# First block's gates: SiLU by ScalarE's table replaced by tanh on ScalarE and a product on VectorE, inside the attention

## Chip, core and metric

The kernel runs on one core of one Trainium2 chip. The metric is the time of one execution in microseconds (us). Engines are TensorE (PE; its weight loads are PEld), VectorE (DVE), ScalarE (ACT), GpSimd (POOL), and SyncE (SP), which issues most DMAs.

## What is computed

Two transformer-like blocks on 512 tokens of width 1024, in float32. Only the end of the first block's mixing matters here:

```python
y_ssm  = s5_mixer(ssm_u, ...) * jax.nn.silu(ssm_z)            # 512 x 512
y_attn = dsa_mixer(q, k, v, q_idx, k_idx, w_idx, ...) * jax.nn.silu(attn_z)   # 512 x 512
y = jnp.concatenate([y_ssm, y_attn], axis=-1) @ w_out[l]
x = x + gate[:, None, :] * y
```

`s5_mixer` is a state space layer that ends in `z * sigmoid(z @ w_glu + b_glu)`; `dsa_mixer` is causal attention with 8 heads of 64 over the 128 keys that an indexer selects for each query. `silu(v)` is `v * sigmoid(v)`, which is also `0.5 * v * (1 + tanh(v / 2))`.

## The kernel before

Activations lie feature-major: 128 features on the partitions, 512 tokens along the free dimension; a tile of that shape is a chunk. Each float32 product is made of three TensorE passes over numbers split into a high and a low part (`w_hi`, `w_lo`; `h_hi`, `h_lo`; `y_hi`, `y_lo`), all by the one matmul helper at L575. Weights come as 1 MB tiles through three buffers `w_raw`; ScalarE rounds a tile to `w_hi`, VectorE subtracts to get `w_lo`. A group is one such tile: two halves of 128 output features, each 24 matmuls of 128x512 into one PSUM bank. Groups rotate through three banks (`GEMM_BANKS`), and `bank_free` tells TensorE that a bank has been read. Nothing is scheduled by a planner: every engine's order is written out by hand, and semaphores tie the engines together.

**The stage of the change** is one loop of 16 steps, j = 0 to 15, that overlaps the attention with the products `attn_z` and `ssm_z`. Step j serves two heads for query tile j // 4, so its keys are 128 wide in steps 0 to 3, 256 in 4 to 7, 384 in 8 to 11 and 512 in 12 to 15.

- TensorE, in step j: `logits(j+1)` (matmuls `bank<-k,q`), `transposes(j)` (L954), which wait for the normalised probabilities, `values(j-1)` (`bank<-pT,v`), then 4 units of the gate products (3 units from step 8 on); a unit is three matmuls. Half 0 of the eight gate halves is done ahead of the loop, the other seven inside. After it come `values(15)` and `out1`, the product with `w_out`, whose first half waits for each of its eight inputs `y` in turn by `counts=(4, 5, 6, 7, 8, 8, 8, 8)` on the number of low parts that are written.
- VectorE, in step j: waits until the exponentials of step j exist, takes reciprocals (L2385), scales the two heads' probabilities (L2387), and then for step j+1 adds the bias to the logits (L2326) and masks them (L2330). Behind these four come the side jobs of the step: two quarters of a weight tile's low part in steps 0, 1, 4, 5, 8, 9, 13 and 14 (`gate_low`, L2340), one round of key selection (`select_keys`, L2208 and L2209) in steps 2, 3, 6 and 7, the products with the gates (`attn_gated`, L2360) in steps 9 and 12, and low parts (L1987) in steps 10 and 13. The four `ssm_gated` (L2373) and their low parts stand behind the loop, and so do those of the last query tile.
- ScalarE, in step j: exponentials for step j+1 (L1546), copies of the turned probabilities (`pT`, L1555), and side jobs: `gate_half` (L1576) copies a finished gate half out of its bank in steps 0, 2, 4, 6, 8, 11, 14 and 15 and frees the bank; `gate_high` rounds half a weight tile (L1567); `gate_silu` (L1582) applies SiLU in place, four chunks `az` at the end of step 7, three chunks `sz` in step 14 and the fourth behind the loop; `high` and `attn_high` write `y_hi`.

The eight inputs of `out1` pass through two buffers `tval`, in the order given by `Y_SSM` and `Y_ATTN`: value a may be written once the low part of value a-2 is done (`new_val`).

```python
Y_SSM, Y_ATTN = [3, 4, 5, 6], [0, 1, 2, 7]
GATE_DONE = {0: 0, 2: 1, 4: 2, 6: 3, 8: 4, 11: 5, 14: 6, 15: 7}   # step: gate half copied there
GATE_LOW  = {0: ..., 1: ..., 4: ..., 5: ..., 8: ..., 9: ..., 13: ..., 14: ...}
```

Of the kernel before, what the change touches and what calls it, by code (L numbers as in the profile page):

```python
# [114 lines left out]
AT = {}  # L115
# [3 lines left out]
    _at += _n  # L119


Y_SSM, Y_ATTN = [3, 4, 5, 6], [0, 1, 2, 7]


def y_ssm(m):

    return AT["y"] + Y_SSM[m]
# [37 lines left out]
def hybrid_blocks(nc, wstream, xT, vecs, consts, head_rows, onehot, rel_bias, ssm_vec, ssm_b, ssm_c, d_skip,  # L165
                  alpha2, decay, reset, outT):
    f32, f32r, i32 = mybir.dt.float32, mybir.dt.float32r, mybir.dt.int32
    ALU, ACT, AX = mybir.AluOpType, mybir.ActivationFunctionType, mybir.AxisListType
# [10 lines left out]
    with ctx:  # L179
# [14 lines left out]
        def sem(name):  # L194
            return ctx.enter_context(nc.semaphore(name))
# [28 lines left out]
        sgb = sb("sgb", [P, 2, SEQ])  # L224
# [64 lines left out]
        bank = [ctx.enter_context(nc.psum_tensor(f"bank{i}", [P, SEQ], f32)) for i in range(8)]  # L289
# [9 lines left out]
        bank_free = [sem(f"bank_free{i}") for i in range(8)]  # L299

        act_val, act_high, act_low = sem("act_val"), sem("act_high"), sem("act_low")
# [5 lines left out]
        cl_zero, bias_spread = sem("cl_zero"), sem("bias_spread")  # L307
        kr_turned, kr_row = sem("kr_turned"), sem("kr_row")
        ki_copied, ki_doubled, wi_ready, wi_row, wi_psum, mod_row, gate_row = sem("ki_copied"), sem("ki_doubled"), sem("wi_ready"), sem("wi_row"), sem("wi_psum"), sem("mod_row"), sem("gate_row")
        az_ready = sem("az_ready")  # L310
        x_act, kr_psum, k_ready, heads_loaded = sem("x_act"), sem("kr_psum"), sem("k_ready"), sem("heads_loaded")
        silu_zero, c_ready, ada_done, mod_ready = sem("silu_zero"), sem("c_ready"), sem("ada_done"), sem("mod_ready")
        setup_trig, trig_ready = sem("setup_trig"), sem("trig_ready")
# [50 lines left out]
        def pbanks(gr):  # L364
            return bank_of(2 * gr.g), bank_of(2 * gr.g + 1)
# [99 lines left out]
        GATE_HALVES = [(gr, half) for name in ("attn_z", "ssm_z") for gr in G[name] for half in range(2)]  # L465
# [5 lines left out]
        GATE_DONE = {0: 0, 2: 1, 4: 2, 6: 3, 8: 4, 11: 5, 14: 6, 15: 7}  # L471
# [101 lines left out]
        def _(pe):  # L573
# [60 lines left out]
            def gemm(gr, kind, hi, lo, k0=0, permuted=False, need=None, between=None, counts=None):  # L634

                gemm_half(gr, 0, kind, hi, lo, k0, permuted, need, counts=counts)
                if between is not None:
                    between()
                gemm_half(gr, 1, kind, hi, lo, k0, permuted, need)
# [236 lines left out]
            gr = G["k"][1]  # L876
# [106 lines left out]
                    unit += 1  # L983
            values(15)
            for w, gr in enumerate(G["out1"]):
                gemm(gr, "fm", y_hi, y_lo, need=AT["y"] if w == 0 else None, counts=(4, 5, 6, 7, 8, 8, 8, 8),
                     between=(lambda: presummed("norm1")) if w == 3 else None)
            pe.wait_ge(pv_read, 4)

# [280 lines left out]
        def _(act):  # L1270
            steps = 0

            def settle(ins):

                nonlocal steps
                steps += 1
                ins.then_inc(act_step, 1)
                act.wait_ge(act_step, steps)
# [289 lines left out]
                if part == 1:  # L1568
                    ins.then_inc(w_high, 1)

            def gate_half(n):

                gr, half = GATE_HALVES[n]
                bk = pbanks(gr)[half]
                act.wait_ge(group_done, 2 * gr.g + half + 1)
                settle(act.copy((az, sz)[n // 4][:, n % 4, :], bank[bk][:, :]))  # L1576
                act.nop().then_inc(bank_free[bk], 1)

            def gate_silu(x, ms):

                for m in ms:
                    ins = act.activation(x[:, m, :], x[:, m, :], ACT.Silu)  # L1582
                ins.then_inc(az_ready, 1)

            def attn_kept(qt):

# [4 lines left out]
            def attn_high(qt):  # L1591

                a = y_attn(qt)
                act.wait_ge(act_val, a + 1)
                act.copy(y_hi[:, 4:8, qt * P:qt * P + P],
                         tval[:, a % 2, :].rearrange("p (c q) -> p c q", q=P)).then_inc(act_high, 1)

            def ssm_high(m):

                high(y_ssm(m), y_hi[:, m, :])  # L1600
# [5 lines left out]
            for j in range(16):  # L1606
                for r in range(2):
                    if j + 1 < 16:
                        probabilities(2 * j + 2 + r)
                    turned_copy(2 * j + r)  # L1610
                if j == 4 or j == 8:
                    attn_kept(j // 4 - 1)
                if j == 15:
                    ssm_high(0)
                    ssm_high(1)
                if j in GATE_DONE:
                    gate_half(GATE_DONE[j])
                if j in GATE_HIGH:
                    gate_high(*GATE_HIGH[j])
                if j == 7:  # L1620
                    gate_silu(az, range(4))
                if j == 9:
                    attn_high(0)
                    attn_high(1)
                if j == 12:
                    attn_high(2)
                if j == 14:
                    gate_silu(sz, range(3))
            gate_silu(sz, (3,))
            ssm_high(2)  # L1630
            ssm_high(3)
            attn_high(3)

# [269 lines left out]
        def _(dve):  # L1903
# [9 lines left out]
            def tt(out, a, b, op):  # L1913
                settle(dve.tensor_tensor(out, a, b, op))  # L1914
# [5 lines left out]
            def stt(out, a, s, b, op0, op1):  # L1920
                settle(dve.scalar_tensor_tensor(out=out, in0=a, scalar=s, in1=b, op0=op0, op1=op1))  # L1921
# [57 lines left out]
            def new_val(a):  # L1979

                if a >= 2:
                    dve.wait_ge(act_low, a - 1)
                return tval[:, a % 2, :]
# [316 lines left out]
            for w, gr in enumerate(G["glu"]):  # L2300
                ahead(gr)
                for half in range(2):
                    m = 2 * w + half
                    if m < 3:
                        select_keys(1)
                    if m == 1:
                        dve.wait_ge(ada_done, 6)
                        dve.tensor_tensor(modv[:, 16:24], bank[4][:, 0:8], vec[:, a0 + 16:a0 + 24], ALU.add)\
                           .then_inc(mod_ready, 1)
                    dve.wait_ge(sig_ready, m + 1)  # L2310
                    tt(z32[:, m, :], sgb[:, m % 2, :], z32[:, m, :], ALU.mult)
                    dve.nop().then_inc(sig_used, 1)
            dve.wait_ge(mod_ready, 5)
            dve.nop().then_inc(copied_dve, 3)
# [30 lines left out]
            def by_tile(x):  # L2345

                return x.rearrange("p (c q) -> p c q", q=P)

            def attn_gated(qt):

                rows = slice(qt * P, qt * P + P)
                dve.wait_ge(az_ready, 1)
                a = y_attn(qt)
                if qt < 2:
                    dve.wait_ge(pv_read, qt + 1)
                    out = q32[:, :, rows]
                else:
                    dve.wait_ge(pv_psum, 8 * qt + 8)
                    out = by_tile(bank[PV_BANK][:, :])
                dve.tensor_tensor(by_tile(new_val(a)), out, az[:, :, rows], ALU.mult).then_inc(act_val, 1)  # L2360
                if qt >= 2:
                    dve.wait_ge(act_val, a + 1)
                    dve.nop().then_inc(pv_read, 1)

            def attn_low(qt):

                rows, a = slice(qt * P, qt * P + P), y_attn(qt)
                low(a, y_lo[:, 4:8, rows], y_hi[:, 4:8, rows], by_tile(tval[:, a % 2, :]))

            def ssm_gated(m):  # L2370

                dve.wait_ge(az_ready, 2 + m // 3)
                dve.tensor_tensor(new_val(y_ssm(m)), z32[:, m, :], sz[:, m, :], ALU.mult).then_inc(act_val, 1)  # L2373

            def ssm_low(m):

                low(y_ssm(m), y_lo[:, m, :], y_hi[:, m, :])
# [3 lines left out]
            for j in range(16):  # L2381
                i = 2 * j
                qt = i // 8
                dve.wait_ge(p_exp, i + 2)
                settle(dve.reciprocal(stat[:, 3, i:i + 2], stat[:, 2, i:i + 2]))  # L2385
                for r in range(2):
                    dve.tensor_scalar(prob(i + r, qt), prob(i + r, qt), stat[:, 3, i + r:i + r + 1], None,  # L2387
                                      ALU.mult).then_inc(p_norm, 1)
                if j + 1 < 16:
                    masked_logits(i + 2)  # L2390
                    masked_logits(i + 3)
                for part in GATE_LOW.get(j, ()):
                    gate_low(*part)
                if j in (2, 3, 6, 7):
                    select_keys(1)
                if j == 9:
                    attn_gated(0)
                    attn_gated(1)
                if j == 10:
                    attn_low(0)  # L2400
                    attn_low(1)
                if j == 12:
                    attn_gated(2)
                if j == 13:
                    attn_low(2)
            for m in range(4):
                ssm_gated(m)
                if m:
                    ssm_low(m - 1)
            attn_gated(3)  # L2410
            ssm_low(3)
            attn_low(3)
# [492 lines left out]
```

## Time and profile before

| | us |
|---|---|
| median of 3 runs (lowest, highest) | 1520.94 (1519.44, 1521.02) |
| the profiled execution's own time | 1518.23 |
| its span in the trace | 1516.4 |
| TensorE busy | 1481.4 |
| VectorE busy | 828.1 |
| ScalarE busy | 604.1 |

The span is what the trace covers; 1.8 us of that execution lie around it. The profiled execution is 2.7 us under the median. A timeline row reads: start, duration, engine, line, operation, what is written and read, shapes, and how many instructions the row merges; in brackets the engine's idle time ahead of it and what ended that. The name of a line can be that of a helper. A window row gives the busy time of each engine in a stretch and `PEclk`, the granted TensorE clock as a share of full speed.

### The profile page before, as it was taken

The page shows a single profiled execution, that of the slowest core. Times are in us where ns is not written, and L with a number is a line of the kernel's source. Part 1 is how long each engine was busy: PE and PEld are TensorE (multiplying, and loading weights), DVE is VectorE, ACT ScalarE, POOL GpSimd, SP SyncE. Part 2 cuts the span into 40 slices and gives each one's busy share as a digit, 9 for nine tenths or more (in the row PEclk, how much of TensorE's full clock was granted, in tenths as well). Part 3 has the DMA queues.
Part 4 walks back from the last instruction along what each step waited for, and adds up shares of the span by engine and source line. Part 5 has one row for each costly group of instructions (what it writes and reads, how often), then busy time and mean ns, then how long its engine had stood idle before and what let it go on. Part 6 is the DMA issues. An engine that isn't in the chain of part 4 may idle for free.

```text
span 1516.4 us, 19843 instructions
## 1 busy us (share of the span) xinstructions
PE 1481.4 (98%) x8104; PEld 1202.5 (79%) x8104; DVE 828.1 (55%) x1359; ACT 604.1 (40%) x918; POOL 22.2 (1%) x39
## 2 busy tenths in 40 slices
PE   7999999999999999999999999999999999999997
PEld 5766967678887887888889777888887888888887
DVE  7978978865647663334346443543448544443234
ACT  4356335663336553334336434332434323232220
POOL 0020100000000000000000000000000000000000
PEclk9999999999999999999999999999999999999998
DMA  8541542043321112122222212222421323232221
GB/s 344 183 112 57 116 161 90 29 167 139 111 80 61 56 56 73 66 84 84 98 105 86 82 56 84 84 98 97 149 101 57 110 84 112 83 111 77 104 98 56
DMA packets 25001, 151.69 MB, mean 100 GB/s; under 512 B 3568, under 2 KB 6240, under 8 KB 8896
## 3 DMA queue, kind: packets, MB, share of 16 engines
q1 hardware_dynamic: 22304, 136.71, 24.9%
q0 software_dynamic: 2608, 13.72, 3.4%
q8 instruction: 64, 1.05, 0.3%
q14 instruction: 25, 0.20, 0.0%
HBM read 143.83 MB, written 7.88 MB: 100 GB/s over the span
## 4 chain that ended last, share of the span: by engine, by line
PE 89%; DVE 6%; ACT 2%; DMA 2%; issue 1%; SPq 0%; DVEq 0%; ACTq 0%
PE bank L575 87%; DMA w_raw<-wstream 2%; PE bank L1022 1%; PE bank L954 1%; DVE score L2224 1%; DVE tmp L1914 0%; DVE w_lo L1961 0%; DVE win_im L1914 0%; DVE win_re L1914 0%; DVE sgb L1921 0%; DVE y_lo L1987 0%; DVE h_lo L1987 0%; DVE tval L2461 0%; ACT w_hi L1291 0%; DVE score L2209 0%
## 5 line engine op out<-in xcount | busy, mean ns | idle before, releaser
L575 PE MATMUL bank<-h_hi,w_hi 128*128 128x512 f32 (+1 forms) x1104 | 438.6, 397 | 5.3 <-DVE h_lo L2743 2.1
L575 PE MATMUL bank<-h_hi,w_lo 128*128 128x512 f32 (+1 forms) x1120 | 437.3, 390 | 0.0
L575 PE MATMUL bank<-h_lo,w_hi 128*128 128x512 f32 (+1 forms) x1104 | 430.9, 390 | 0.0
L1961 DVE TENSOR_TENSOR w_lo<-w_raw,w_hi 128x2048 fp32r<-128x2048 f32 (+2 forms) x104 | 234.6, 2255 | 250.6 <-ACT w_hi L1291 249.3
L1291 ACT CAST w_hi<-w_raw 128x2048 fp32r<-128x2048 f32 (+2 forms) x108 | 202.7, 1876 | 139.0 <-PE bank L575 132.5
L575 PEld LDWEIGHTS bank<-h_hi,w_hi 128*128 128x128 f32 (+1 forms) x1104 | 207.3, 188 | 61.7 <-issue 17.1
L575 PEld LDWEIGHTS bank<-h_hi,w_lo 128*128 128x128 f32 (+1 forms) x1120 | 210.4, 188 | 45.1
L575 PEld LDWEIGHTS bank<-h_lo,w_hi 128*128 128x128 f32 (+1 forms) x1104 | 207.3, 188 | 41.7 <-issue 0.2
L575 PE MATMUL bank<-y_hi,w_hi 128*128 128x512 f32 x272 | 108.9, 400 | 1.9 <-DVE y_lo L1987 1.9
L575 PE MATMUL bank<-y_hi,w_lo 128*128 128x512 f32 x272 | 106.1, 390 | 0.0
L575 PE MATMUL bank<-y_lo,w_hi 128*128 128x512 f32 x272 | 105.9, 389 | 0.0
L575 PE MATMUL bank<-w_hi,h_hi 128*128 128x256 f32 x352 | 101.3, 288 | 0.0
L575 PE MATMUL bank<-w_lo,h_hi 128*128 128x256 f32 x352 | 99.5, 283 | 0.0
L575 PE MATMUL bank<-w_hi,h_lo 128*128 128x256 f32 x352 | 99.5, 283 | 0.0
L1661 ACT ACTIVATE sgb<-bank 128x512 f32<-128x512 f32 x40 | 23.9, 598 | 151.0 <-PE bank L575 151.0
L575 PE MATMUL bank<-f_hi,w_lo 128*128 128x512 f32 (+1 forms) x220 | 76.2, 347 | 0.0
L575 PEld LDWEIGHTS bank<-w_hi,h_hi 128*128 128x128 f32 x352 | 67.4, 191 | 6.2 <-issue 6.1
L575 PE MATMUL bank<-f_hi,w_hi 128*128 128x512 f32 (+1 forms) x196 | 69.8, 356 | 0.0
L575 PE MATMUL bank<-f_lo,w_hi 128*128 128x512 f32 (+1 forms) x196 | 69.4, 354 | 0.0
L575 PEld LDWEIGHTS bank<-w_lo,h_hi 128*128 128x128 f32 x352 | 67.5, 192 | 0.0
L575 PEld LDWEIGHTS bank<-w_hi,h_lo 128*128 128x128 f32 x352 | 67.5, 192 | 0.0
L575 PEld LDWEIGHTS bank<-y_hi,w_hi 128*128 128x128 f32 x272 | 51.1, 188 | 16.3 <-DVE y_lo L1987 3.6
(401 smaller groups left out, 1817.5 us busy)
## 6 DMA issues: line engine op xcount, KB each, us to landing
w_raw<-wstream SPq DMA_DIRECT2D x119, 1024.0 KB, 4.8
w_raw<-wstream SPq DMA_DIRECT2D x4, 768.0 KB, 4.1
bias_rows<-bias_table POOLq DMA_DIRECT2D x1, 2560.0 KB, 11.2
xr<-xT SPq DMA_DIRECT2D x4, 512.0 KB, 5.0
bias<-bias_rows POOLq DMA_DIRECT2D x1, 2048.0 KB, 12.8
xr<-xT SPq DMA_DIRECT2D x1, 2048.0 KB, 8.7
x_saved<-xr POOLq DMA_DIRECT2D x1, 2048.0 KB, 10.4
xr<-x_saved POOLq DMA_DIRECT2D x1, 2048.0 KB, 8.1
```

The source lines that it names most:

```text
L575: return pe.matmul(out, lhsT, rhs, start=start, stop=stop)
L954: ins = pe.transpose(bank[PT_BANKS[r]][:, s * P:s * P + P], prob(i, qt)[:, s * P:s * P + P], ident)
L1022: ins = pe.transpose(bank[ST_BANKS[t % 2]][:, j * P:j * P + P], lg[:, n % 2, j, kb * P:kb * P + P], ident)
L1291: act.copy(hi_of(s)[:, 0:kt, :], w_raw[:, i % RAW_SLOTS, 0:kt, :]).then_inc(w_high, 1)
L1661: act.activation(sgb[:, m % 2, :], bank[bk][:, :], func).then_inc(bank_free[bk], 1)
L1961: dve.tensor_tensor(w_low_of(s)[:, 0:kt, :], w_raw[:, i % RAW_SLOTS, 0:kt, :], hi_of(s)[:, 0:kt, :].bitcast(f32), ALU.subtract).then_inc(w ...
L2224: dve.scalar_tensor_tensor(out=score[:, qt, 0:w], in0=sgb[:, i % 2, 0:w], scalar=wi[:, qt, h:h + 1], in1=score[:, qt, 0:w], op0=ALU.mult, ...
```

## The change

ScalarE no longer copies the gate halves and applies SiLU later. `gate_tanh` writes `tanh(v / 2)` straight from the bank in the same steps in which the copy stood; the SiLU activations of this stage are gone. VectorE's new `gate_silu` computes `(tanh + 1) * v` with the bank as second input, one step later (steps 1, 3, 5, 7, 9, 12 and 15, and once behind the loop), and frees the bank. The factor 0.5 goes into `attn_gated` and, for the state space chunks, into the product that ends `s5_mixer`; both become scalar-tensor-tensor operations. The rounds of key selection stand in steps 1, 3, 5 and 7 instead of 2, 3, 6 and 7. `ssm_gated(0)` and `(1)` and their low parts move into steps 11 to 14, so two more of the eight inputs of `out1` are ready when the loop ends, and the `tval` order and the first of the `counts` follow.

```diff
--- before.py
+++ after.py
@@ -119,7 +119,7 @@
     _at += _n
 
 
-Y_SSM, Y_ATTN = [3, 4, 5, 6], [0, 1, 2, 7]
+Y_SSM, Y_ATTN = [2, 4, 5, 6], [0, 1, 3, 7]
 
 
 def y_ssm(m):
...
@@ -983,7 +983,7 @@
                     unit += 1
             values(15)
             for w, gr in enumerate(G["out1"]):
-                gemm(gr, "fm", y_hi, y_lo, need=AT["y"] if w == 0 else None, counts=(4, 5, 6, 7, 8, 8, 8, 8),
+                gemm(gr, "fm", y_hi, y_lo, need=AT["y"] if w == 0 else None, counts=(3, 5, 6, 7, 8, 8, 8, 8),
                      between=(lambda: presummed("norm1")) if w == 3 else None)
             pe.wait_ge(pv_read, 4)
 
@@ -1568,19 +1568,12 @@
                 if part == 1:
                     ins.then_inc(w_high, 1)
 
-            def gate_half(n):
+            def gate_tanh(n):
 
                 gr, half = GATE_HALVES[n]
-                bk = pbanks(gr)[half]
                 act.wait_ge(group_done, 2 * gr.g + half + 1)
-                settle(act.copy((az, sz)[n // 4][:, n % 4, :], bank[bk][:, :]))
-                act.nop().then_inc(bank_free[bk], 1)
-
-            def gate_silu(x, ms):
-
-                for m in ms:
-                    ins = act.activation(x[:, m, :], x[:, m, :], ACT.Silu)
-                ins.then_inc(az_ready, 1)
+                act.activation((az, sz)[n // 4][:, n % 4, :], bank[pbanks(gr)[half]][:, :], ACT.Tanh, scale=0.5)\
+                   .then_inc(tanh_ready, 1)
 
             def attn_kept(qt):
 
@@ -1610,24 +1603,21 @@
                     turned_copy(2 * j + r)
                 if j == 4 or j == 8:
                     attn_kept(j // 4 - 1)
-                if j == 15:
-                    ssm_high(0)
-                    ssm_high(1)
                 if j in GATE_DONE:
-                    gate_half(GATE_DONE[j])
+                    gate_tanh(GATE_DONE[j])
                 if j in GATE_HIGH:
                     gate_high(*GATE_HIGH[j])
-                if j == 7:
-                    gate_silu(az, range(4))
                 if j == 9:
                     attn_high(0)
                     attn_high(1)
+                if j == 11:
+                    ssm_high(0)
                 if j == 12:
                     attn_high(2)
-                if j == 14:
-                    gate_silu(sz, range(3))
-            gate_silu(sz, (3,))
-            ssm_high(2)
+                if j == 13:
+                    ssm_high(1)
+                if j == 15:
+                    ssm_high(2)
             ssm_high(3)
             attn_high(3)
 
@@ -2308,7 +2298,7 @@
                         dve.tensor_tensor(modv[:, 16:24], bank[4][:, 0:8], vec[:, a0 + 16:a0 + 24], ALU.add)\
                            .then_inc(mod_ready, 1)
                     dve.wait_ge(sig_ready, m + 1)
-                    tt(z32[:, m, :], sgb[:, m % 2, :], z32[:, m, :], ALU.mult)
+                    stt(z32[:, m, :], sgb[:, m % 2, :], 0.5, z32[:, m, :], ALU.mult, ALU.mult)
                     dve.nop().then_inc(sig_used, 1)
             dve.wait_ge(mod_ready, 5)
             dve.nop().then_inc(copied_dve, 3)
@@ -2349,7 +2339,7 @@
             def attn_gated(qt):
 
                 rows = slice(qt * P, qt * P + P)
-                dve.wait_ge(az_ready, 1)
+                dve.wait_ge(az_ready, 4)
                 a = y_attn(qt)
                 if qt < 2:
                     dve.wait_ge(pv_read, qt + 1)
@@ -2357,7 +2347,8 @@
                 else:
                     dve.wait_ge(pv_psum, 8 * qt + 8)
                     out = by_tile(bank[PV_BANK][:, :])
-                dve.tensor_tensor(by_tile(new_val(a)), out, az[:, :, rows], ALU.mult).then_inc(act_val, 1)
+                dve.scalar_tensor_tensor(out=by_tile(new_val(a)), in0=out, scalar=0.5, in1=az[:, :, rows],
+                                         op0=ALU.mult, op1=ALU.mult).then_inc(act_val, 1)
                 if qt >= 2:
                     dve.wait_ge(act_val, a + 1)
                     dve.nop().then_inc(pv_read, 1)
@@ -2369,8 +2360,18 @@
 
             def ssm_gated(m):
 
-                dve.wait_ge(az_ready, 2 + m // 3)
+                dve.wait_ge(az_ready, 5 + m)
                 dve.tensor_tensor(new_val(y_ssm(m)), z32[:, m, :], sz[:, m, :], ALU.mult).then_inc(act_val, 1)
+
+            def gate_silu(n):
+
+                gr, half = GATE_HALVES[n]
+                bk, x = pbanks(gr)[half], (az, sz)[n // 4][:, n % 4, :]
+                dve.wait_ge(tanh_ready, n + 1)
+                dve.scalar_tensor_tensor(out=x, in0=x, scalar=1.0, in1=bank[bk][:, :], op0=ALU.add,
+                                         op1=ALU.mult).then_inc(az_ready, 1)
+                dve.wait_ge(az_ready, n + 1)
+                dve.nop().then_inc(bank_free[bk], 1)
 
             def ssm_low(m):
 
@@ -2391,7 +2392,9 @@
                     masked_logits(i + 3)
                 for part in GATE_LOW.get(j, ()):
                     gate_low(*part)
-                if j in (2, 3, 6, 7):
+                if j - 1 in GATE_DONE:
+                    gate_silu(GATE_DONE[j - 1])
+                if j in (1, 3, 5, 7):
                     select_keys(1)
                 if j == 9:
                     attn_gated(0)
@@ -2399,14 +2402,20 @@
                 if j == 10:
                     attn_low(0)
                     attn_low(1)
+                if j == 11:
+                    ssm_gated(0)
                 if j == 12:
+                    ssm_low(0)
                     attn_gated(2)
                 if j == 13:
                     attn_low(2)
-            for m in range(4):
-                ssm_gated(m)
-                if m:
-                    ssm_low(m - 1)
+                    ssm_gated(1)
+                if j == 14:
+                    ssm_low(1)
+            ssm_gated(2)
+            gate_silu(GATE_DONE[15])
+            ssm_gated(3)
+            ssm_low(2)
             attn_gated(3)
             ssm_low(3)
             attn_low(3)
```

## Rows read from the trace of the kernel before

**Rows 1.** The page: chain that ended last, shares by engine

```profile
PE 89%; DVE 6%; ACT 2%; DMA 2%; issue 1%; SPq 0%; DVEq 0%; ACTq 0%
```

**Rows 2.** Windows: the loop up to step 9, and one microsecond in step 9

```profile
240.00:280.00 40.00, 40.00 (x221) 27.33 (x221) 32.72 (x101) 24.36 (x64) 0.00 (x0) 1.00 0.15 54
...
283.00:284.00 1.00, 1.00 (x8) 0.67 (x8) 0.96 (x4) 0.20 (x2) 0.00 (x0) 0.50 0.00 0
```

**Rows 3.** Timeline of PE, from 247 to 324 us

```profile
247.91 0.44 PE L954 MATMUL bank<-cst,sgb 128*128 128x128 f32 x2
...
279.60 0.92 PE L575 MATMUL bank<-k,q 64*128 64x384 f32 x4
282.52 1.16 PE L954 MATMUL bank<-cst,sqb 128*128 128x128 f32 x6 [2.00 <-DVE sqb L2387]
...
287.95 0.92 PE L575 MATMUL bank<-k,q 64*128 64x384 f32 x4
...
292.67 1.13 PE L575 MATMUL bank<-k,q 64*128 64x512 f32 x4
...
303.82 1.09 PE L954 MATMUL bank<-cst,sqb 128*128 128x128 f32 x8
...
309.26 1.09 PE L954 MATMUL bank<-cst,sgb 128*128 128x128 f32 x8
...
314.25 1.09 PE L954 MATMUL bank<-cst,sqb 128*128 128x128 f32 x8 [0.61 <-DVE sqb L2387]
...
318.57 1.09 PE L575 MATMUL bank<-pT,v 128*64 128x128 f32 x16
...
323.98 0.50 PE L575 MATMUL bank<-y_hi,w_hi 128*128 128x512 f32 x1 [0.70 <-DVE y_lo L1987]
```

**Rows 4.** Timeline of ACT, from 275 to 279 us: table changes

```profile
275.33 1.28 ACT L1582 ACT_TABLE_LOAD   x1
...
278.83 1.28 ACT L1546 ACT_TABLE_LOAD   x1
```

**Rows 5.** Timeline of DVE, from 246 to 324 us

```profile
246.27 0.16 DVE L2385 RECIPROCAL stat<-stat 128x2 f32<-128x2 f32 x1
...
282.71 0.61 DVE L2326 SCALAR_TENSOR_TENSOR sgb<-bank,stat,bias 128x384 f32<-128x384 f32 x1
...
287.38 0.15 DVE L2385 RECIPROCAL stat<-stat 128x2 f32<-128x2 f32 x1
...
302.53 0.17 DVE L2385 RECIPROCAL stat<-stat 128x2 f32<-128x2 f32 x1 [0.28 <-ACT sqb L1546]
...
308.53 0.15 DVE L2385 RECIPROCAL stat<-stat 128x2 f32<-128x2 f32 x1
...
313.52 0.15 DVE L2385 RECIPROCAL stat<-stat 128x2 f32<-128x2 f32 x1
...
322.40 0.69 DVE L2360 TENSOR_TENSOR tval<-bank,az 128x512 f32<-128x512 f32 x1
323.23 1.29 DVE L1987 TENSOR_TENSOR y_lo<-tval,y_hi 128x512 fp32r<-128x512 f32 x2
```

**Rows 6.** Groups by line and shape over the whole span (busy us, mean ns)

```profile
L1921 DVE SCALAR_TENSOR_TENSOR la<-la,lb 128x512 f32<-128x512 f32 x4 | 2.8, 693 | 4.8 <-ACT lb L1804 4.8
...
L1661 ACT ACTIVATE sgb<-bank 128x512 f32<-128x512 f32 x40 | 23.9, 598 | 151.0 <-PE bank L575 151.0
```

**Rows 7.** Groups by line and shape of DVE, 232 to 326 us

```profile
L2208 DVE MAX8 small<-score 128x8 f32<-128x512 f32 x5 | 3.4, 688 | 0.0
L2209 DVE MATCH_REPLACE8 score<-small,score 128x512 f32<-128x512 f32 x5 | 3.4, 677 | 0.0
...
L2387 DVE TENSOR_SCALAR sgb<-sgb,stat 128x128 f32<-128x128 f32 x4 | 1.0, 283 | 0.1
```

**Rows 8.** Waits of PE over the whole span (total, times, longest)

```profile
PE bank L575 <- DVE h_lo L2743: 2.1, 1, 2.1
PE bank L575 <- DVE w_lo L1961: 1.9, 1, 1.9
```

More of the change, by code:

```diff
@@ L309, in hybrid_blocks @@
         ki_copied, ki_doubled, wi_ready, wi_row, wi_psum, mod_row, gate_row = sem("ki_copied"), sem("ki_doubled"), sem("wi_ready"), sem("wi_row"), sem("wi_psum"), sem("mod_row"), sem("gate_row")
-        az_ready = sem("az_ready")
+        tanh_ready, az_ready = sem("tanh_ready"), sem("az_ready")
         x_act, kr_psum, k_ready, heads_loaded = sem("x_act"), sem("kr_psum"), sem("k_ready"), sem("heads_loaded")
```

## The prediction

> **What bounds the kernel now.** I read the chain that ended last first: 89% of it is TensorE [rows 1], so a change outside TensorE counts only where it removes or adds a pause of TensorE. The windows show which engine is next: in the 40 us up to step 9 TensorE is busy all the time and VectorE 32.7 us, 82%, ScalarE 24.4 us [rows 2]. The reserve is VectorE's, and it is thin. Then TensorE's timeline, step by step, with VectorE's beside it. In three places TensorE pauses in or just behind this loop.
>
> Step 9: its transposes start after 2.00 us of idleness, at 282.52, and from one logits to the next it takes 287.95 - 279.60 = 8.35 us, where the following step takes 292.67 - 287.95 = 4.72 [rows 3]. So 3.63 us are lost: 2.00 idle, and some 1.6 because the granted clock then stands at 0.50, the lower of its two levels (1.2 instead of 2.4 GHz) [rows 2]. The cause is ScalarE: a table load of 1.28 us at 275.33, four SiLU, another load at 278.83 [rows 4], and the exponentials for step 9 behind them. Step 15: 314.25, idle 0.61, some 0.65 late by the row before; this one is VectorE's doing. Behind the loop: from the last `values` at 318.57 to the fourth input of `out1` at 323.98 it is 5.41 us [rows 3], where 1.03 for the values and three units of 0.68 would be 3.1.
>
> **What goes.** The SiLU block of step 7 and both loads round it: 3.63 us, if nothing takes its place. The copy out of the bank becomes a tanh out of the bank; the nearest row, another function from bank to SBUF, takes 0.598 [rows 6], as the copy did, and it lies beside other work.
>
> **What comes, on VectorE.** `gate_silu` is a scalar-tensor-tensor with an immediate; such a one over 512 columns takes 0.693 [rows 6], and with the wait for its own end I charge 0.73. One with its second input in a bank and an immediate scalar is not in the trace; the bounds are 0.60 (the pitch of back-to-back operations, half of the 1.29 of two [rows 5]) and 0.80; I take 0.73. A round of selection is 0.688 + 0.677 [rows 7] and a small load between, 1.51 in all. A moved `ssm_gated` or low part costs 0.60 of VectorE's time.
>
> What counts is when the first head of step j+1 is normalised, against when TensorE comes to its transposes. From the start of the reciprocal to those transposes it takes 314.25 - 313.52 = 0.73 us in steps where TensorE waits [rows 3, 5]; with 128 columns the scaling is 0.283 [rows 7], so about 0.55. Side jobs added ahead of the reciprocal move it one for one once the reserve is used.
>
> Step 1: before, the reciprocal starts at 246.27 [rows 5], the result is there at 246.82, TensorE comes at 247.91 [rows 3]: reserve 1.09. Added: 0.73 + 1.51 = 2.24. Pause **1.15**. Three more steps are read in the same way from their own pairs of rows: step 3, reserve 0.36, added 0.73, pause **0.37**; step 5, reserve 1.04, added 2.24, pause **1.20**; step 7, reserve 0.0, added 0.73, pause **0.73**. Taking a selection round out of steps 2 and 6 gives nothing back, since they had reserve.
>
> Step 9 has to be rebuilt, as its rows are disturbed. VectorE goes from first bias to reciprocal in 287.38 - 282.71 = 4.67 us [rows 5], with two gate_low parts and two `attn_gated`. It can begin some 0.94 after the logits start (their 0.92 us [rows 3]). So 0.94 + 4.67 + 0.68 = 6.29 after the logits, and TensorE comes to the transposes 4.72 + 0.86 = 5.58 after them: late by 0.71 already, once the SiLU block no longer hides it. With `gate_silu` 0.73 more: **1.44**.
>
> Step 11: one `ssm_gated`, covered by VectorE's wait for ScalarE there. Step 12: the reciprocal starts at 302.53 after 0.28 of idleness [rows 5], so VectorE was free at 302.25; plus 0.73 + 0.60, then 0.73, is 304.31, against 303.82 [rows 3]: **0.49**. Step 13: the reciprocal at 308.53 and the transposes at 309.26 [rows 3, 5] touch already; added is one `ssm_gated`, 0.60, and 0.16 since VectorE now begins the step late: **0.76**. Step 14: pause 0.65 before, a low part of 0.60 more: **1.25**.
>
> The sum: 1.15 + 0.37 + 1.20 + 0.73 + 1.44 + 0.49 + 0.76 + 1.25 = 7.39 us of pauses in place of 3.63 + 0.65 = 4.28. The loop gets 3.1 us longer.
>
> **Behind the loop** something comes back. Count from the last `values` (318.57 before). Half 7 has just ended; the tanh, no longer behind SiLU work, runs from 0.1 to 0.7, `gate_silu` to 1.45, `ssm_gated(3)` to 2.15, and low part 2 ends at 2.8. `attn_gated(3)` waits for that and starts at 2.9; its spacing to the next low part was 323.23 - 322.40 = 0.83 [rows 5], so low part 3 ends at 4.45 and TensorE takes the fourth input at 4.5, the rest at 5.2 without another wait. Before it was 5.41: **0.9** less. The next weight tile of `out1` is rounded behind this and has some 4 us to spare, and the reload of `x` starts as soon as the last logits are masked, as before; both move with the loop.
>
> Net: 7.39 - 4.28 - 0.9 = **+2.2 us**. Against the profiled execution: span 1516.4 to 1518.6, its own time 1518.23 to 1520.4. The median of the runs is 2.7 us above that execution, so 1520.94 + 2.2 = **1523.1**. About 0.2%, 3.0 us, is what a measurement of this kernel can tell from no change, so this lies inside it.
>
> The products that end `s5_mixer` and `attn_gated` change from tensor-tensor to scalar-tensor-tensor with an immediate: 0.693 against 0.69 for `attn_gated` in the timeline [rows 5, 6], nothing. The Trainium skill (Vector Engine (DVE) Microarchitecture Reference, section Points that are easy to get wrong) says that a scalar-tensor-tensor with two non-bf16 inputs in SBUF runs at half throughput. Rows 6 are such an operation at 693 ns, so the trace speaks against it; by that rule the two `attn_gated` of step 9 would cost 1.4 us more and the sum would be +3.6.
>
> **Rivals.**
>
> *VectorE's additions fit in.* If the reserve is larger than I read, as when the reciprocal's chain overlaps better, the pauses of the loop vanish and the gain stays: -3.63 - 0.9 to -5.2 with step 15's, so 1515.7 to 1516.4. It decides at step 1: the selection round and the gate together would have to fit into 1.1 us [rows 3, 5]. Against it stands that step 15 pauses before by the very sum that I use. 0.08.
>
> *The clock falls.* A pause may bring the granted clock down again, at 1.6 us each time. Before, 2.00 us did [rows 2, 3]; elsewhere TensorE waits up to 1.9 and 2.1 us [rows 8]. My longest are 1.44, 1.25 and 1.20, in steps 9, 14 and 5. One fall gives 1524.7, two 1526.3: slower. It decides if one of them comes near 2 us. 0.15.
>
> *tanh needs a table of its own.* Then the loads do not go but multiply: two of 1.28 us [rows 4] around each tanh. ScalarE idles for some 1.7 us ahead of the exponentials, and VectorE's extra work hides more; the rest shows in step 12 (about 0.8) and the last tanh's load behind the loop (1.3): 1525.2. For the whole change not to do what it says it would have to be this. 0.05. The Trainium skill (ScalarE: Activation LUTs, section Table sets: the hidden batching unit) lists tanh in the set of exp, which would exclude this; no run so far shows it.
>
> **How the numbers follow.** The forecast itself has 0.72. Its unknowns are the price of `gate_silu` (0.60 to 0.80 at six counting places: -0.8 to +0.4), the estimate of step 9 (0.3 either way), and the runs of before, which differ by 1.6 us among themselves. So its own range is 1521 to 1525, and of its 0.72 some 0.20 lies over +3.0. Faster 0.07, same 0.52, slower 0.20 + 0.15 + 0.05 and rounding, 0.41. The range takes in the falls of the clock: 1520.8 to 1526.4.
>
> **What the profile will show.** No table load between the one ahead of the loop and the one for the square root. No 2.00 us pause in step 9, and steps 1, 5, 9, 13 and 14 each with TensorE's transposes waiting for L2387 of VectorE by 0.8 to 1.4 us; those would say that VectorE is the bound. VectorE near 90% busy in the loop. `out1`'s first two inputs back to back. If the transposes of step 2 start without a wait, my reading of the reserves is wrong; if the granted clock shows 0.50 in the loop, the second rival is at work.

## The result and the profile after

| | before | after |
|---|---|---|
| median of 14 runs each, us (lowest, highest) | 1519.07 (1517.06, 1521.70) | 1522.66 (1521.38, 1524.07) |
| ratio to before, 95% interval | | 1.0022 (1.0015 to 1.0030) |
| profiled execution, its own time, us | 1518.23 | 1524.07 |
| its span, us | 1516.4 | 1522.3 |

The change makes the kernel slower by 1.5 to 3.0 per thousand, 3.4 us at the middle (the medians lie 3.59 apart); 2.2 were forecast. (With 14 runs the median of before is 1.9 us lower than that of the three runs shown at first.)

TensorE's timeline of the changed kernel, at the places that answer to [rows 3]; in brackets is the idle time ahead of a row and what ended it:

```profile
242.38 0.49 PE L575 MATMUL bank<-k,q 64*128 64x128 f32 x4
242.80 0.44 PE L954 MATMUL bank<-cst,sgb 128*128 128x128 f32 x2
...
250.07 0.49 PE L575 MATMUL bank<-k,q 64*128 64x128 f32 x4
251.75 0.52 PE L954 MATMUL bank<-cst,sgb 128*128 128x128 f32 x2 [1.18 <-DVE sgb L2388]
...
260.95 0.70 PE L954 MATMUL bank<-cst,sgb 128*128 128x128 f32 x4 [0.40 <-DVE sgb L2388]
...
271.55 0.70 PE L954 MATMUL bank<-cst,sgb 128*128 128x128 f32 x4 [1.13 <-DVE sgb L2388]
...
282.43 0.88 PE L954 MATMUL bank<-cst,sgb 128*128 128x128 f32 x6 [0.78 <-DVE sgb L2388]
...
290.83 0.92 PE L575 MATMUL bank<-k,q 64*128 64x384 f32 x4
293.34 0.88 PE L954 MATMUL bank<-cst,sgb 128*128 128x128 f32 x6 [1.60 <-DVE sgb L2388]
...
309.15 1.09 PE L954 MATMUL bank<-cst,sqb 128*128 128x128 f32 x8 [0.69 <-DVE sqb L2388]
...
315.35 1.09 PE L954 MATMUL bank<-cst,sgb 128*128 128x128 f32 x8 [0.73 <-DVE sgb L2388]
...
320.94 1.09 PE L954 MATMUL bank<-cst,sqb 128*128 128x128 f32 x8 [1.18 <-DVE sqb L2388]
...
325.25 1.09 PE L575 MATMUL bank<-pT,v 128*64 128x128 f32 x16
326.28 0.50 PE L575 MATMUL bank<-y_hi,w_hi 128*128 128x512 f32 x1
...
327.08 0.40 PE L575 MATMUL bank<-y_hi,w_hi 128*128 128x512 f32 x1
...
329.91 0.50 PE L575 MATMUL bank<-y_hi,w_hi 128*128 128x512 f32 x1 [0.70 <-DVE y_lo L1977]
```

The pause of 2.00 us in step 9 that ScalarE made is gone. In its place TensorE pauses at eight points, seven of them new and the one of step 15 grown from 0.61 to 1.18 us idle, and each is ended by L2388, VectorE's scaling of the probabilities. They stand ahead of the transposes of steps 2, 4, 6, 8, 10, 13, 14 and 15: in each case one step behind the step that got more side jobs. What TensorE loses at one is a little more than the idle time shown: the transposes start 1.68 us after the logits ahead of them where they otherwise start 0.42 after (242.80 - 242.38), so 1.26 are lost at the first. Read in this way the eight are 1.26, 0.47, 1.21, 0.85, 1.67, 0.76, 0.80 and 1.25 us, 8.27 in all.

VectorE's timeline in step 1 shows the cause. It is the stretch that ended with the reciprocal at 246.27 in [rows 5]:

```profile
247.65 1.29 DVE L2330 TENSOR_TENSOR w_lo<-w_raw,w_hi 128x512 fp32r<-128x512 f32 x2
248.86 0.68 DVE L2371 SCALAR_TENSOR_TENSOR az<-az,bank 128x512 f32<-128x512 f32 x1
249.69 0.69 DVE L2198 MAX8 small<-score 128x8 f32<-128x512 f32 x1
250.41 0.09 DVE L2199 MATCH_VALUE_LOAD score<-small,score 128x8 f32 x1
250.49 0.68 DVE L2199 MATCH_REPLACE8 score<-small,score 128x512 f32<-128x512 f32 x1
251.20 0.17 DVE L2386 RECIPROCAL stat<-stat 128x2 f32<-128x2 f32 x1
```

The gate's product takes 0.68 us and occupies the engine for 0.83 (249.69 - 248.86), since VectorE waits for its end to signal the bank. Without it and the selection round the reciprocal would start at 248.86. Two windows of the changed kernel, columns as in [rows 2]: the steps up to 9, and steps 12 to 14.

```profile
242.00:293.00 51.00, 46.25 (x256) 30.79 (x255) 42.16 (x123) 26.21 (x74) 0.00 (x0) 1.00 0.12 42
303.00:321.00 18.00, 15.40 (x106) 10.41 (x104) 17.31 (x38) 11.76 (x24) 0.00 (x0) 1.00 0.10 22
```

In the first VectorE is busy 83% of the time, in the second 96% (TensorE 91% and 86%). The granted clock is 1.00 in both, so 2.4 GHz, and in the microseconds between them too: no pause of the loop brought it down. The table load for the exponential stands at 237.21, ahead of the loop, and the next one, for the square root, at 329.68; tanh and the exponential run between them without a load, so both are served by the same table (grouped by line, 238 to 329 us, a window that still catches the end of the first load):

```profile
L1575 ACT ACTIVATE az<-bank 128x512 f32<-128x512 f32 x4 | 2.4, 600 | 0.0
...
L1595 ACT ACT_TABLE_LOAD x1 | 1.3, 1283 | 0.2 <-ACT sgb L1539 0.2
```

From the second logits to the fourth input of `out1` the changed kernel takes 329.91 - 242.38 = 87.53 us, before 84.19 (323.98 - 239.79): 3.34 more. That is the measured change. The second logits of the kernel before start here:

```profile
239.79 0.49 PE L575 MATMUL bank<-k,q 64*128 64x128 f32 x4
```

The other 2.6 us by which the two profiled spans differ lie ahead of the loop, where the changed kernel's trace has the granted clock at its lower level twice, near 29 and 70 us, and that of before not at all; a second trace of the kernel before has one of them too, near 68 us, and starts the loop 1 us later. From the fourth input on the two traces agree to 0.1 us.

### The profile page after: what moved, and what is told of

Its sections match the earlier page's. It is cut to its first block, busy times and chain, and to the rows that moved or that the text cites. A ratio compares the mean times of both kernels' runs of the same rounds, so it can differ in the third digit from the quotient of the medians.

```text
span 1522.3 us, 19840 instructions
## 1 busy us (share of the span) xinstructions
PE 1484.0 (97%) x8104; PEld 1204.2 (79%) x8104; DVE 832.9 (55%) x1367; ACT 595.7 (39%) x907; POOL 22.1 (1%) x39
## 4 chain that ended last, share of the span: by engine, by line
PE 88%; DVE 7%; ACT 2%; issue 1%; DMA 1%; SPq 0%; DVEq 0%; ACTq 0%
PE bank L575 86%; DMA w_raw<-wstream 1%; PE bank L1022 1%; DVE score L2214 0%; DVE score L2199 0%; DVE sgb L2316 0%; DVE w_lo L2330 0%; DVE small L2198 0%; PE bank L954 0%; DVE tmp L1904 0%; DVE w_lo L1951 0%; DVE win_im L1904 0%; DVE win_re L1904 0%; DVE sgb L1911 0%; DVE h_lo L1977 0%
```

## Experiments

The stretch above, from the second logits to the fourth input of `out1`, is called the stretch; for the two kernels that were traced twice it repeats within 0.1 us (84.19 and 84.16; 86.53 and 86.61), so it resolves what the timed ratios, with intervals of some 2 per thousand, do not.

### Selection back to steps 2, 3, 6 and 7

```diff
-                if j in (1, 3, 5, 7):
+                if j in (2, 3, 6, 7):
                     select_keys(1)
```

> The changed kernel with the rounds of key selection back in steps 2, 3, 6 and 7. If VectorE's side jobs ahead of the reciprocal make the pauses one for one: the pauses ahead of the transposes of steps 2 and 6 (1.18 and 1.13 us idle in the changed kernel) are gone, since 1.21 + 0.83 fits the reserve of some 2.3 us of a step, steps 2 and 6 themselves stay without a pause in steps 3 and 7 of TensorE, and the loop is 2.4 us shorter than in the changed kernel, about 1 us longer than before: ratio to before 1.0007. If the pauses come from the gates' products alone (their banks, their place), the move does nothing: ratio 1.002 as for the changed kernel.

Ratio 1.0016 (1.0007 to 1.0026). The pauses ahead of the transposes of steps 2 and 6 are gone and the six others stayed within 0.02 us: 5.80 instead of 8.27. The stretch is 84.97 us, 2.56 less than in the changed kernel and 0.78 more than before. Here are TensorE's rows in place of those at 250.07 and 251.75:

```profile
247.59 0.49 PE L575 MATMUL bank<-k,q 64*128 64x128 f32 x4
248.01 0.44 PE L954 MATMUL bank<-cst,sgb 128*128 128x128 f32 x2
```

So by the stretch, putting back the selection rounds alone, which had been moved by one step, from steps with room to steps without, undoes 2.56 of the net 3.34 us. It removes 2.47 of the 8.27 us of pauses; the pauses gone from steps 9 and 15 (4.28) and the shorter way behind the loop (0.75) pay for 5.0 of the 5.80 that are left. The timed runs do not show the 2.56: 0.78 us more than before would be a ratio of 1.0005, just under the interval of 1.0007 to 1.0026, while 1.0016 is near the 1.002 that the other case in the expectation gave. The trace decides that the two pauses went, and its execution was, with 1518.97 us, the fastest of the ten. What the other nine lost is not known.

### State space chunks behind the loop

```diff
-Y_SSM, Y_ATTN = [2, 4, 5, 6], [0, 1, 3, 7]
+Y_SSM, Y_ATTN = [3, 4, 5, 6], [0, 1, 2, 7]
...
-                if j == 11:
-                    ssm_gated(0)
...
+            ssm_gated(0)
+            ssm_gated(1)
+            ssm_low(0)
             ssm_gated(2)
+            ssm_low(1)
             gate_silu(GATE_DONE[15])
             ssm_gated(3)
```

> The changed kernel with the state space chunks gated and split behind the loop, as before, but ahead of the last gate_silu. If side jobs count one for one: the pauses ahead of the transposes of steps 13, 14 and 15 shrink by 0.6 us each (0.76, 0.80, 1.25 to about 0.15, 0.15, 0.65), and nothing is paid behind the loop, since VectorE is idle for 3.2 us there: 1.8 us less than the changed kernel, ratio to before about 1.001. If the early chunks are what shortens the way from the last values to the fourth input of out1 (5.41 to 4.66 us), that comes back and takes 0.75 us of it: ratio 1.0015.

> The same kernel as ssm_behind, for a second trace. Its timed ratio of 1.003 is above the 1.0015 that its loop and tail account for. If falls of the granted clock near 326 and 442 us belong to this kernel, they show again; if they fall at random, at least one of the two is absent, and the pauses of the loop are the same as in the first trace to 0.05 us.

Ratio 1.0030 (1.0019 to 1.0041). The loop did as expected: the pauses for steps 13, 14 and 15 are 0.25, 0.23 and 0.64 us (second trace 0.24, 0.23, 0.65), 1.69 less. But from the last values to the fourth input it takes 5.42 us again (5.44), as before and not 4.66, so in this order of VectorE the early chunks are what shortens that way. They are not the only means: the kernel before without SiLU takes 4.73 us with no chunk moved, and the kernel of the fifth experiment 4.65 with only the first chunk in step 15. What the changed kernel adds behind the loop, the last `gate_silu`, is what the early chunks make up for here. VectorE's rows show why the way is long in this kernel: it idles 1.38 us behind the first two chunks, because ScalarE rounds the first only after its two last copies of probabilities, and `gate_silu(7)` starts 0.8 us after its tanh is done.

```profile
317.73 1.29 DVE L2363 TENSOR_TENSOR tval<-z,sz 128x512 f32<-128x512 f32 x2 [0.21 <-DVE sz L2370]
320.40 0.69 DVE L1976 TENSOR_TENSOR y_lo<-tval,y_hi 128x512 fp32r<-128x512 f32 x1 [1.38 <-ACT y_hi L1299]
```

And there is a cost I had not expected. TensorE waits 1.08 us and then 0.68 for the third and fourth input; at the fourth the granted clock falls, in both traces:

```profile
324.65 0.50 PE L575 MATMUL bank<-y_hi,w_hi 128*128 128x512 f32 x1 [1.08 <-DVE y_lo L1976]
...
326.31 0.79 PE L575 MATMUL bank<-y_hi,w_hi 128*128 128x512 f32 x1 [0.68 <-DVE y_lo L1976]
326.90 0.63 PE L575 MATMUL bank<-y_lo,w_hi 128*128 128x512 f32 x1
```

A window over a microsecond of it has 0.50:

```profile
327.00:328.00 1.00, 1.00 (x4) 0.80 (x3) 0.00 (x0) 0.96 (x3) 0.56 (x1) 0.50 0.06 25
```

From the fourth input to the first product after the second block's last norm, 814.7 us in the kernels before and after, it takes 816.3 us in the second trace, where this is the only fall: 1.6 more. With the stretch of 86.61, 2.4 more than before, it makes 4.0 us more than before, 1.0026, inside the interval. The fall near 442 us in the first trace is absent from the second, so that one does not belong to the kernel.

### The gates' products left out

```diff
-                dve.scalar_tensor_tensor(out=x, in0=x, scalar=1.0, in1=bank[bk][:, :], op0=ALU.add,
-                                         op1=ALU.mult).then_inc(az_ready, 1)
-                dve.wait_ge(az_ready, n + 1)
+                dve.nop().then_inc(az_ready, 1)
```

> The changed kernel without VectorE's eight products of tanh + 1 and the bank: the gates stay tanh, so that part of the computation is left out. By the forecast's sum each product costs TensorE 0.85 us wherever the reserve is used up: pauses of about 0.4, 0, 0.35, 0, 0.75 us ahead of the transposes of steps 2, 4, 6, 8 and 10, 0 for step 13, 0.6 to 0.8 for 14 and 1.25 for 15; the loop is some 4.5 us shorter than in the changed kernel and the way behind it 0.7 shorter: ratio to before about 0.9985. If instead the tanh or ScalarE's new order sets the pauses, they stay, and the ratio is above 1.001.

Ratio 0.9994 (0.9985 to 1.0004). The pauses are 0.42, 0, 0.38, 0.02 and 0.71 us for steps 2, 4, 6, 8 and 10, 0 for 13, then 0.73 and 1.25: 3.5 in all, every one within 0.05 of what was expected (with 0.85 us for a product, the price read in the changed kernel, not the forecast's 0.73). The stretch is 82.13 us, 2.06 less than before. ScalarE's tanh and its new order therefore cost nothing that shows in the loop; VectorE's eight products of 0.83 us account for 4.8 of the 8.27. (The shares of products, selection rounds and chunks, 4.8, 2.5 and 1.7, add up to more than 8.27, since they use up the same reserves.) The ratio is less good than the stretch alone would make it (0.9986), though inside the interval. This trace has one more fall of the clock, near 437 us; that the other runs had it too is not shown.

### The kernel before without SiLU

```diff
-                for m in ms:
-                    ins = act.activation(x[:, m, :], x[:, m, :], ACT.Silu)
-                ins.then_inc(az_ready, 1)
+                act.nop().then_inc(az_ready, 1)
```

> The kernel before, with ScalarE's eight SiLU (and with them their table loads) left out, so the gates are not SiLU. The pause of 2.00 us ahead of the transposes of step 9 and the fall of the granted clock behind it go. By the forecast's rebuilding of step 9 a pause of 0.7 us then shows ahead of the transposes of step 10, hidden before; without it the step before takes 4.7 us. So the loop gains 3.6 - 0.7 = 2.9 us, and what stands behind it some 1 us: ratio 0.9975. A rival: the 0.7 is not there and the gain is 3.6 + 1: ratio 0.997.

> The kernel before, for a second trace. If the pause of 2.00 us in step 9 always brings the clock down, step 9 takes 8.35 us again; if not, it takes some 6.8.

Ratio 0.9976 (0.9966 to 0.9985). Step 9 takes 4.72 us instead of 8.35, and a pause appears that the trace before did not have: TensorE loses 0.74 us ahead of the transposes of step 10, where 0.71 had been worked out. The stretch is 80.64 us, 3.55 less than before: 3.63 - 0.74 in the loop and 0.68 behind it, where some 1 us had been expected. This is the whole value of taking SiLU off ScalarE with every other job left in its place, at a price of nothing. The second trace of the kernel before has the pause (1.99 us) and the fall of the clock in step 9 again.

### Side jobs placed by the reserve of each step

```diff
+        SILU_AT = {1: 0, 4: 1, 5: 2, 6: 3, 10: 4, 12: 5, 15: 6}
...
-                if j - 1 in GATE_DONE:
-                    gate_silu(GATE_DONE[j - 1])
-                if j in (1, 3, 5, 7):
+                if j in (2, 3, 6, 7):
                     select_keys(1)
+                if j == 15:
+                    ssm_gated(0)
+                if j in SILU_AT:
+                    gate_silu(SILU_AT[j])
                 if j == 9:
                     attn_gated(0)
-                    attn_gated(1)
                 if j == 10:
-                    attn_low(0)
-                    attn_low(1)
+                    attn_gated(1)
                 if j == 11:
-                    ssm_gated(0)
+                    attn_low(0)
+                    attn_low(1)
```

The rest of the chunks stand behind the loop as in the second experiment, and on ScalarE `ssm_high(0)` goes ahead of the last two copies and `attn_high(1)` into step 10.

> The changed kernel with every side job of VectorE placed by the reserve of its step: selection in 2, 3, 6, 7; gate_silu 0 to 6 in steps 1, 4, 5, 6, 10, 12, 15; attn_gated 0 and 1 in 9 and 10, their low parts in 11; the state space chunks behind the loop, the first rounded ahead of the last copies of ScalarE. If the reserve is what counts (about 2.3, 2.3, 1.9, 2.1, 2.3, 2.3, 2.0, 1.5, 1.7, 1.9, 1.3, 1.5, 1.7, 0.7 us in steps 1 to 14), the pauses ahead of the transposes come to 0.1 to 0.2 us in steps 10, 13 and 14 and 0.6 in 15, 1.1 in all instead of 8.3, and with 4.7 us from the last values to the fourth input of out1 the stretch from the second logits to there is 80.4 us (before 84.2, changed 87.5): ratio 0.9975. If tanh on ScalarE with the product on VectorE is itself the mistake, it stays above 0.999.

Ratio 0.9978 (0.9969 to 0.9987). The stretch is 80.40 us, as worked out, against 84.19 before and 87.53 in the changed kernel. The pauses ahead of the transposes of steps 10, 13, 14 and 15 are 0.14, 0.32, 0.22 and 0.66 us, 1.34 in all; for the 0.32, made in step 12, I had estimated too little, since `attn_gated(2)` has to wait for the end of its own product and `gate_silu` for its. From the last values to the fourth input it takes 4.65 us. TensorE never pauses in the 40 us up to step 9, though VectorE is busier than before (35.0 instead of 32.7 us of [rows 2]):

```profile
240.00:280.00 40.00, 40.00 (x222) 27.43 (x221) 35.03 (x107) 22.09 (x64) 0.00 (x0) 1.00 0.16 54
```

So tanh on ScalarE with the product on VectorE can be faster than before; the steps that the change used for it were the mistake. What the tanh form itself is worth against a mere change of order is not shown: this kernel also takes `attn_gated(1)` out of step 9, and no run leaves SiLU in place and spreads its eight activations, or the side jobs of the kernel before, over other steps.

### The bank signalled a step later, and a quarter of the tile moved

From the kernel of the last experiment:

```diff
-                dve.wait_ge(az_ready, n + 1)
-                dve.nop().then_inc(bank_free[bk], 1)
...
+                if j - 1 in SILU_AT:
+                    gate_freed(SILU_AT[j - 1])
                 dve.wait_ge(p_exp, i + 2)
...
-                    8: ((3, 0), (3, 1)), 9: ((3, 2), (3, 3)), 13: ((4, 0), (4, 1)), 14: ((4, 2), (4, 3))}
+                    8: ((3, 0), (3, 1)), 9: ((3, 2), (3, 3)), 13: ((4, 0), (4, 1)), 14: ((4, 2),), 15: ((4, 3),)}
```

> As balanced, but VectorE signals the free bank at the start of its next step instead of waiting for the product's own end (0.15 us of each gate_silu's 0.83), and a quarter of the last weight tile's low part goes from step 14 to step 15. If the waits and quarters cost as the sum says: pauses ahead of the transposes of 13 and 14 near 0, of 15 near 0.1, the stretch another 0.7 us shorter, 79.7 us, ratio 0.997; if the quarter in step 15 comes back behind the loop, from the last values to the fourth input it takes 5.2 us instead of 4.7 and the gain is 0.2.

Ratio 0.9972 (0.9963 to 0.9981), median 1514.98 us of 11 runs, below the kernels before and after. The stretch is 79.79 us, 0.61 less than in the kernel ahead of it; the pauses are 0.14, 0.05, 0.19 and 0.42, and the quarter in step 15 did not come back behind the loop (4.47 us). The last two are larger than expected (near 0 and 0.1). Of the 0.42, 0.28 us is no longer VectorE's doing: it idles that long for ScalarE's exponential. The wait for a product's own end is saved only where another job follows in the same step, as in step 12 (0.32 to 0.05). Where `gate_silu` comes last, the wait stands at once at the head of the next step, and the product still occupies 0.83 us (247.42 to 248.25). The timed intervals of the two overlap, so that the second is the better one rests on its trace.

## Why the prediction was right, and where it was off

The side and the mechanism were right: VectorE, with a thin reserve, becomes the bound, and the gain of 3.63 us in step 9 is taken back in small pauses. That the time came out within 0.4 us (1523.1 forecast, 1522.66 measured) is partly luck: the forecast started from a median of before that was 1.9 us too high, and its change was 1.1 us (by the stretch) to 1.4 us (by the medians) too small. By its steps, as forecast and as measured:

| step that gets the jobs | 1 | 3 | 5 | 7 | 9 | 12 | 13 | 14 | sum |
|---|---|---|---|---|---|---|---|---|---|
| forecast, us | 1.15 | 0.37 | 1.20 | 0.73 | 1.44 | 0.49 | 0.76 | 1.25 | 7.39 |
| measured, us | 1.26 | 0.47 | 1.21 | 0.85 | 1.67 | 0.76 | 0.80 | 1.25 | 8.27 |

- **The term that was mis-sized** is `gate_silu` with the wait for its own end, 0.73 us; it measured 0.83, and 0.93 in step 9, where the product that follows waits for it (290.53 to 291.46, [0.25 idle]). I had added 0.04 for the wait and forgotten that here a signal of the bank stands between. That is 0.1 in each of steps 1, 3, 7 and 12, and most of the 0.23 in step 9; step 5 had 0.1 more reserve than I read, so nothing shows there. In step 12 the same wait and signal stand behind `attn_gated` (307.58 to 308.41, 0.83 us for a product of 0.68). Before, they lay hidden in the 0.28 us of idleness ahead of the reciprocal: I took VectorE as free at 302.25, the end of the product, where it was free 0.15 later. With `gate_silu`'s 0.1 that is 0.25 of the 0.27 missed there.
- **What goes** was 3.63 + 0.65 us as read, and the experiment without SiLU confirmed the first and the hidden 0.71 (0.74) of step 9.
- **Behind the loop**: -0.9 forecast, 5.41 to 4.66 measured, -0.75. The parts are: SiLU gone 0.68 less, as in the kernel before without it (4.73); with the last `gate_silu` behind the loop 0.7 more, by difference (5.42 in the second experiment); the early chunks 0.76 less, at the price of 1.7 us of pauses.
- **The sum**: 8.27 - 4.28 - 0.75 = 3.24, and 3.34 measured. The unknowns that I named allowed at most 2.2 + 0.4 + 0.3 = 2.9, so the change lies above them, and outside the 0.2% that I had as the likeliest; with 14 runs of each the interval is clear of no change.
- **The rivals**: the additions did not fit in. The clock did not fall in the loop at pauses of up to 1.60 us, though it did behind the loop in one of the experiments at less. tanh needed no table of its own: the Trainium skill (ScalarE: Activation LUTs, section Table sets: the hidden batching unit) lists it with exp, and the trace agrees, with no load between 238.5 and 329.6 us, tanh and the exponential alternating.
- **The signs**: TensorE's transposes wait for VectorE behind steps 1, 5, 9, 13 and 14 as said, by 0.73 to 1.60 us instead of 0.8 to 1.4. From 242 to 326 us VectorE is busy 83% of the time and not near 90%; the 96% of steps 12 to 14 is where it has no room left.
- The Trainium skill's half throughput for a scalar-tensor-tensor with two non-bf16 inputs in SBUF (Vector Engine (DVE) Microarchitecture Reference, section Points that are easy to get wrong) is not what this kernel does: the two `attn_gated` of step 9, now of that kind, take 1.29 us together; before, as tensor-tensor, it was 1.28.

```profile
291.46 1.29 DVE L2350 SCALAR_TENSOR_TENSOR tval<-q,az 128x512 f32<-128x512 f32 x2 [0.25 <-DVE sz L2371]
```

## What to carry to other kernels

In a loop where one engine's side jobs stand ahead of what the bound engine waits for, work out each step's reserve (the time from the bound engine's product to its next need, less the fixed chain), and place the jobs by it: here the average load of 82% hid that, beside the side jobs that it had already, step 7 had 0.0 us left and step 1 1.1, and the same side jobs cost 8.3 us of pauses in one order and 1.3 in another. Moving work that costs nothing in one step to the next is a change like any other. And look for what a stall hides: with SiLU gone, 0.7 us of VectorE's came to light.

## What the runs showed of the hardware that was not expected

Pauses shorter than I thought can bring the granted clock down, and the same pause does not always do it. I had taken some 2 us as the mark from the kernel before. The ten traces, of eight kernels, show this of single idle stretches of TensorE, each followed by a fall to 0.50 or not:

| idle, us | where | fell in |
|---|---|---|
| 2.14 | second block, at 1138.70 before | 10 of 10 traces |
| 2.00 | step 9 of the kernel before | 2 of 2 |
| 1.9 | at 68.60 before | 6 of 10 |
| 1.6 | ahead of the transposes of step 10 | 0 of 4 |
| 1.08, then 0.68 (0.70) | third and fourth input, second experiment | 2 of 2 |
| 0.93, then 0.97 | at 435.99 and 437.68 before | 2 of 10 |

```profile
68.60 0.47 PE L575 MATMUL bank<-h_hi,w_hi 128*128 128x512 f32 x1 [1.90 <-DVE w_lo L1961]
...
1138.70 0.47 PE L575 MATMUL bank<-h_hi,w_hi 128*128 128x512 f32 x1 [2.14 <-DVE h_lo L2743]
```

So the length of a pause alone does not decide it, and two traces are few to call the fall of the second experiment its own. Where TensorE is the bound a fall costs 1.6 us. The falls that come and go are a part of the 3 to 6 us by which the runs of one kernel differ: in the first experiment the fastest run (1518.97 us) has a mean granted clock of 0.995, the slowest (1525.17) 0.992. What decides whether a given pause brings the clock down stays open.
